# State-space layer: swapped diagonal product, a second home for R, and an output projection one column tile at a time

## The reference, cut to what matters

```
def ssd_mixer(h, w_in, ...):                       # 32 heads of 64, 4 groups of 8 heads, state 128
    z, xbc, dt = split(h @ w_in)
    xs, bm, cm = split(silu(dwconv_centered(xbc)))
    y_f, s_f = ssd_chunked(xs, dt[0], a[0], bm, cm, init_f)
    y_b, s_b = ssd_chunked(flip(xs), flip(dt[1]), a[1], flip(bm), flip(cm), init_b)
    y = y_f + flip(y_b) + xs * d_skip
    y = rmsnorm(y * silu(z), norm_g)
    return y @ w_out, s_f, s_b

def ssd_chunked(x, dt, a, bm, cm, init_state):     # chunks of 128 tokens
    acs  = cumsum(dt * a)
    lmat = exp(where(lower, acs_i - acs_j, -inf))
    wmat = (cc @ bc.T) * lmat * dt
    y_diag = wmat @ xc
    chunk_states = bc.T @ (exp(acs_end - acs) * dt * xc)
    starts = scan(state * exp(acs_end) + chunk_states)
    y_off  = (cc @ starts) * exp(acs)
    return y_diag + y_off, final
```

## Time and profile before

| | us |
|---|---|
| median of 3 runs | 2035.67 (2027.53 to 2037.62) |
| profiled execution | 2033.17 |
| its span, first to last instruction | 2031.3 |
| TensorE busy in it | 1898.1 |
| VectorE, GpSimd, ScalarE busy | 1049.7, 1204.2, 607.1 |

### The profile page before, as it was taken

One profiled execution on the slowest core, in us unless ns is written; L12 is line 12 of the kernel. 1 busy time (PEld: TensorE's weight loads), 2 busy tenths in 40 slices (PEclk: granted clock), 3 DMA queues, 4 the chain that ended last, 5 costly groups with the idle time before them and its releaser, 6 DMA issues. The chain is left out here.

```text
span 2031.3 us, 33370 instructions
## 1 busy us (share of the span) xinstructions
PE 1898.1 (93%) x12777; PEld 1797.1 (88%) x12777; DVE 1049.7 (52%) x1631; ACT 607.1 (30%) x1152; POOL 1204.2 (59%) x869
## 2 busy tenths in 40 slices
PE   4988879999999999989999999986999999999997
PEld 3867768999999999989999899975899999999997
DVE  4445565455246416455675766677426632561553
ACT  4223322122012102233574646474102210220221
POOL 2422325777777677756545555422687767777764
PEclk8989989999999999999999999988999999999998
DMA  8531314242433424433333323221422222222211
GB/s 296 203 116 46 109 34 168 89 154 75 143 108 120 133 85 153 148 104 89 112 94 104 120 78 114 83 77 53 121 73 73 72 71 75 72 73 66 78 56 70
DMA packets 256185, 208.61 MB, mean 103 GB/s; under 512 B 7352, under 2 KB 235741, under 8 KB 255453
## 3 DMA queue, kind: packets, MB, share of 16 engines
q1 hardware_dynamic: 256093, 207.32, 32.3%
HBM read 196.63 MB, written 10.67 MB: 102 GB/s over the span
## 5 line engine op out<-in xcount | busy, mean ns | idle before, releaser
L899 POOL TENSOR_SCALAR w_hi<-raw 128x512 fp32r<-128x512 f32 (+1 forms) x432 | 653.4, 1529 | 801.1 <-PE ps L933 728.0
L903 POOL TENSOR_TENSOR w_lo<-raw,w_hi 128x512 fp32r<-128x512 f32 (+1 forms) x432 | 557.6, 1312 | 0.0
L933 PE MATMUL ps<-h_hi,w_hi 128*128 128x320 f32 (+1 forms) x1688 | 415.0, 326 | 5.2 <-DVE h_lo L2159 3.1
L933 PE MATMUL ps<-h_lo,w_hi 128*128 128x320 f32 (+1 forms) x1688 | 393.4, 314 | 0.0
L933 PE MATMUL ps<-h_hi,w_lo 128*128 128x320 f32 (+1 forms) x1688 | 391.6, 313 | 0.0
L933 PEld LDWEIGHTS ps<-h_hi,w_hi 128*128 128x128 f32 x1688 | 288.0, 192 | 26.5 <-issue 21.2
L933 PEld LDWEIGHTS ps<-h_hi,w_lo 128*128 128x128 f32 x1688 | 289.2, 191 | 0.0
L933 PEld LDWEIGHTS ps<-h_lo,w_hi 128*128 128x128 f32 x1688 | 288.4, 191 | 0.2 <-issue 0.2
L2054 DVE SCALAR_TENSOR_TENSOR xT<-ps,mod,xT 128x128 f32 (+1 forms) x112 | 56.6, 547 | 275.1 <-PE ps L933 269.5
L933 PE MATMUL ps<-g_hi,w_hi 128*128 128x322 f32 (+1 forms) x816 | 190.7, 315 | 7.0 <-DVE g_lo L2115 7.0
L933 PE MATMUL ps<-g_lo,w_hi 128*128 128x322 f32 (+1 forms) x816 | 189.3, 313 | 0.0
(11 more groups left out here) (334 smaller groups left out, 2879.1 us busy)
## 6 DMA issues: line engine op xcount, KB each, us to landing
raw<-in_ffn_w_up SPq DMA_DIRECT2D x88, 512.0 KB, 3.8
ada<-in_ada_w SPq DMA_DIRECT2D x36, 1024.0 KB, 6.4
raw<-in_ssd_w_in SPq DMA_DIRECT2D x40, 512.0 KB, 4.1
R<-scr_acs SPq DMA_DIRECT2D x40, 512.0 KB, 4.7
raw<-in_ffn_w_down SPq DMA_DIRECT2D x32, 512.0 KB, 3.8
ada_att<-in_ada_w SPq DMA_DIRECT2D x12, 1024.0 KB, 8.1
raw<-in_att_w_in SPq DMA_DIRECT2D x16, 512.0 KB, 7.2
raw<-in_ssd_w_out SPq DMA_DIRECT2D x16, 512.0 KB, 3.9
```

Source lines behind the costliest of these rows:

```text
L899: nc.gpsimd.tensor_scalar(w_hi[j % 2][:, a_:b_, :], raw[j][:, a_:b_, :], 1.0, None, ALU.mult).then_inc(w_hi_done, 1)
L903: ins = nc.gpsimd.tensor_tensor(w_lo[j % 2][:, a_:b_, :], raw[j][:, a_:b_, :], w_hi[j % 2][:, a_:b_, :].bitcast(F32), ALU.subtract)
L933: ins = mm(out[:, cols], w[slot][:, k, :], x[:, cols], start=first and k == 0 and i == 0, stop=last and k == n - 1 and i == 2)
```

## The change

Four edits, all in layer 1's mixer.

1. The diagonal product is swapped: 64 columns of xdt are the weights and R moves (128 columns), so the result has channels on partitions, even heads on 0 to 63, odd heads on 64 to 127. y1 (skip term and the two state products) is no longer added by VectorE but multiplied by the identity into the same bank, and the bank goes straight into the gate product. The event yT is gone; yo stands before cb of its chunk, and VectorE makes the skip term there (for chunk 0 in cb).
2. R has a second home: R_mid (in the last four tiles of yg) for odd n up to 13, R_last (in the last four tiles of h_lo's place) for n = 16 and 18. Rows are loaded two chunks ahead; R_last waits for the last projection tile.
3. ScalarE's part of cb is an event of its own, seg, two slots earlier (in the slot of cb for chunk 1 of group 3).
4. Column tiles 2 to 7 of the output projection are done one at a time (both halves of the channels, weight buffers 0 and 1), in PSUM slots m % 4; the sums of squares and the broadcast for the norm stand between the matmuls of tile 2, after k = 1 and k = 5, in banks 6 and 7.

```diff
                 put(*slots[at], "csf", g, c)
+            if c:
+                put(*slots[at - 1], "yo", g, c)
+            put(*slots[at - (0 if (g, c) == (GROUPS - 1, 1) else 2)], "seg", g, c)
             put(*slots[at + 2], "yd", g, c)
-            if c:
-                put(*slots[at + 3], "yo", g, c)
-            put(*slots[at + 6], "yT", g, c)
         put(*slots[10], "stT", g)
...
+        def aligned(at_):
+
+            return -(-at_ // 32) * 32
+
+        R_mid = at("R_mid", [P, 2, GH, P], F32, aligned(g_at + 12 * W * 4))[0]
+        R_last = at("R_last", [P, 2, GH, P], F32, aligned(h_at + 12 * W * 4))[0]
+        N_MID, N_ALL = CHUNKS * (GROUPS - 1), CHUNKS * GROUPS
+
+        def row_home(n):
+
+            if n < N_MID:
+                return (R, R_mid)[n % 2]
+            return (R, R_last)[(n - N_MID) % 2]
+
+        def row_before(n):
+
+            return n - 1 if n == N_MID else n - 2
+
+        def rows_in(n, d_):
+
+            if n < N_MID:
+                return (R_in, RM_in)[n % 2][d_], 16 * (n // 2 + 1)
+            i = n - N_MID
+            return (RL_in[d_], 16 * (i // 2 + 1)) if i % 2 else (R_in[d_], 16 * (-(-N_MID // 2) + i // 2 + 1))
+
         def h2(name, n, offset):
...
                 g, c = divmod(n, CHUNKS)
-                if n and d_ == 0:
-                    sp.wait_ge(R_used, n)
-                elif n:
-                    sp.wait_ge(ssd_mm, SSD_USE[("yd", (n - 1) // CHUNKS, (n - 1) % CHUNKS)] + 1)
+                if n == N_MID + 1:
+                    sp.wait_ge(mm_done, T_E + 40)
+                elif n >= 2:
+                    sp.wait_ge(R_used, 2 * row_before(n) + 1 + d_)
                 src = scr_acs[c, 32 * d_ + g * GH:32 * d_ + (g + 1) * GH, :]
-                sp.dma_start(R[:, d_, :, :], src.partition_broadcast(P)).then_inc(R_in[d_], 16)
+                sp.dma_start(row_home(n)[:, d_, :, :], src.partition_broadcast(P)).then_inc(rows_in(n, d_)[0], 16)
...
                         state_loads(ev[1] + 1)
-                    if ev[0] == "yd" and ev[1:] != (GROUPS - 1, CHUNKS - 1):
-                        for d_ in range(2):
-                            row_loads(CHUNKS * ev[1] + ev[2] + 1, d_)
+                    if ev[0] == "yd":
+                        n = CHUNKS * ev[1] + ev[2]
+                        after = () if n == N_MID - 2 else (n + 1, n + 2) if n in (N_MID - 1, N_MID) else (n + 2,)
+                        for i in after if n != N_MID - 1 else (n + 1,):
+                            for d_ in range(2):
+                                if i < N_ALL:
+                                    row_loads(i, d_)
                     if ev[0] == "stT":
...
                         for r in range(GH):
-                            ins = mm(bank(b, HD, r * HD), R[:, d_, r, :], xdt[:, d_, r * HD:(r + 1) * HD],
-                                     start=(d_, r) == (0, 0), stop=(d_, r) == (1, GH - 1), skip_group_check=True)
-                        ins.then_inc((R_used, ssd_mm)[d_], 1)
+                            half = HD * (r % 2)
+                            ins = mm(bank(b, P, (r // 2) * P)[half:half + HD, :], xdt[:, d_, r * HD:(r + 1) * HD],
+                                     row_home(CHUNKS * g + ev[2])[:, d_, r, :], start=d_ == 0 and r < 2, stop=False, skip_group_check=True)
+                        ins.then_inc(R_used, 1)
+                    pe.wait_ge(y_done, 5 * g + ev[2] + 1)
+                    for q_ in range(4):
+                        ins = mm(bank(b, P, q_ * P), y1[ev[2] % 2][:, q_ * P:(q_ + 1) * P], ident, start=False,
+                                 stop=q_ == 3, skip_group_check=True)
+                    ins.then_inc(ssd_mm, 1)
                 elif kind == "yo":
...
                         mm(bank(b), cT[g % 2][:, cols], src, start=True, stop=True).then_inc(ssd_mm, 1)
-                elif kind == "yT":
-                    pe.wait_ge(y_done, 5 * g + ev[2] + 1)
-                    b = ssd_begin(ev)
-                    for q_ in range(4):
-                        ins = tr(bank(b, P, q_ * P), y1[ev[2] % 2][:, q_ * P:(q_ + 1) * P], ident)
-                    ins.then_inc(ssd_mm, 1)
                 elif kind == "stT":
...
-            def y_rb():
-                pe.wait_ge(yr_dg, 1)
-                rb(diag).then_inc(yr_rb, 1)
-
-            def so_pair(i):
+            def y_sums_row(k):
+
+                if k == 1:
+                    pe.wait_ge(y_added, 15)
+                    for c in range(CHUNKS):
+                        ins = mm(bank(6, 1, c), y_sums[:, chunk_col(c):chunk_col(c) + P], ones[:, 0:1], start=True,
+                                 stop=True)
+                    ins.then_inc(y_ss, 1)
+                if k == 5:
+                    pe.wait_ge(yr_dg, 1)
+                    rb(diag, 6).then_inc(yr_rb, 1)
+
+            def so_tile(m):
                 for part in range(2):
-                    for half in range(2):
-                        pe.wait_ge(w_split, 4 * i + (T_O + 2 * part + half + 1))
-                        if part == 0:
-                            pe.wait_ge(acc_free_dve, 2 * i + (half + dve_accs(A_O) - 2))
-                        steps(half, half, y_of(part), range(KD), first=part == 0, last=part == 1).then_inc(mm_done, 1)
+                    pe.wait_ge(w_split, so_done(m) - 1 + part)
+                    if part == 0:
+                        if m == 2:
+                            pe.wait_ge(*ssd_end(("yd", GROUPS - 1, CHUNKS - 1)))
+                            pe.wait_ge(*ssd_end(("stT", GROUPS - 1, 1)))
+                        elif m == 3:
+                            pe.wait_ge(rbs_done, 1)
+                        else:
+                            pe.wait_ge(acc_free_dve, dve_accs(A_O) + m - 4)
+                    steps(part, so_slot(m), y_of(part), range(KD), first=part == 0, last=part == 1,
+                          after=y_sums_row if (m, part) == (2, 0) else None).then_inc(mm_done, 1)
             for k in range(12, 16):
                 y_part(k)
-            pe.wait_ge(y_added, 15)
-            for c in range(CHUNKS):
-                ins = mm(bank(6, 1, c), y_sums[:, chunk_col(c):chunk_col(c) + P], ones[:, 0:1], start=True, stop=True)
-            ins.then_inc(y_ss, 1)
-            y_rb()
-            with pe.Fori(1, 4) as i:
-                so_pair(i)
+            for m in range(2, KD):
+                so_tile(m)
             ffn(1, T_F1, A_F1)
...
                     A_(st_f[1][:, :] if d_ == 0 else st_b[:, 3, :], bank(b), ACT.Copy).then_inc(ssd_free_act, 1)
-                elif kind == "cb":
+                elif kind == "seg":
                     n = 5 * g + ev[2]
                     c = ev[2]
                     for d_ in range(2):
-                        act.wait_ge(R_in[d_], 16 * (n + 1))
+                        act.wait_ge(*rows_in(n, d_))
+                        R_ = row_home(n)
                         for r in range(GH):
                             i = 32 * d_ + GH * g + r
-                            ins = A_(R[:, d_, r, :], R[:, d_, r, :], ACT.Relu, bias=acs[:, c, i:i + 1], scale=-1.0)
+                            ins = A_(R_[:, d_, r, :], R_[:, d_, r, :], ACT.Relu, bias=acs[:, c, i:i + 1], scale=-1.0)
                         step(ins)
                         step.wait()
-                        A_(R[:, d_, :, :], R[:, d_, :, :], ACT.Exp, scale=-1.0).then_inc(seg_exp, 1)
+                        A_(R_[:, d_, :, :], R_[:, d_, :, :], ACT.Exp, scale=-1.0).then_inc(seg_exp, 1)
                 elif kind == "stT":
...
+            def skip_term(g, c):
+
+                if c >= 2:
+                    dve.wait_ge(ssd_mm, SSD_USE[("yd", g, c - 2)] + 1)
+                elif g:
+                    dve.wait_ge(ssd_mm, SSD_USE[("yd", g - 1, 4)] + 1)
+                return tt(h64(y1[c % 2][:, :]), h64(x_tok[g % 2][:, c, :]), bc(d_bc[:, GH * g:GH * (g + 1)], 2, HD),
+                          ALU.mult)
+
             n_id = 0
...
                     tt(cbm[:, :, :], bc(bank(b, P), 1, 2), masks, ALU.mult).then_inc(ssd_free_dve, 1)
+                    if c == 0:
+                        skip_term(g, 0).then_inc(y_done, 1)
                     if n:
-                        dve.wait_ge(ssd_mm, SSD_USE[("yd", g, c - 1) if c else ("yd", g - 1, 4)] + 1)
+                        dve.wait_ge(R_used, 2 * n)
                     else:
...
                         dve.wait_ge(seg_exp, 2 * n + d_ + 1)
-                        tt(R[:, d_, :, :], R[:, d_, :, :], bc(cbm[:, d_, :], 1, GH), ALU.mult).then_inc(W_done, 1)
+                        R_ = row_home(n)
+                        tt(R_[:, d_, :, :], R_[:, d_, :, :], bc(cbm[:, d_, :], 1, GH), ALU.mult).then_inc(W_done, 1)
                 elif kind == "yd":
-                    n = 5 * g + c
-                    y_ = y1[c % 2][:, :]
-
-                    if c >= 2:
-                        dve.wait_ge(ssd_mm, SSD_USE[("yT", g, c - 2)] + 1)
-                    elif g:
```

(35 more changed lines are left out.)

17 lines of the change are left out of this document (11 added, 6 removed).

## The result

| kernel | median of the runs, us | profiled execution, us | span, us | mean granted clock |
|---|---|---|---|---|
| before, beside it | 2036.64 (4 runs) | 2033.17 | 2031.3 | 0.970 |
| after | 2001.97 (1999.62 to 2008.77, 4 runs) | 1999.62 | 1997.7 | 0.977 |

The ratio is 0.984, with an interval of 0.9815 to 0.9865: faster, by 1.6% and clear of the noise, though by less than 2%. The forecast was 2007.5, in a range of 1996 to 2026; as a ratio, 2007.5/2035.67 = 0.986, just inside the upper end of that interval. The gain in the medians is 34.7 us, in the two profiled executions 33.6, and the forecast had 28.2.

A forecast was written before the change was run, and what follows sets the result against it. TensorE was taken to bound the projection tiles, a chain through several engines the tail. Profiled 2033.2 - 16.8 (product) - 13.4 (tail) + 2 (waits) = 2005.0; with 2.5 for the median 2007.5 us, range 1996 to 2026.

The forecast's parts named there:

- Part 1: Swapped diagonal product on TensorE: column halves overlap, 55 ns a record, burst 1.76 us plus 0.2 for edges, before 3.52.
- rival A: Swapped diagonal product: column halves don't overlap, 107 ns a record, 2035 us in all, no change; chance 0.12.
- The drain at a change of tiling mode: At each swapped burst's edges: 0.11 us seen leaving; at 0.40 an edge the first stretch would win 9 us less.
- Part 2: Identity matmuls replace transposes on TensorE, 0.88 us against 0.44; with the swap 1.12 us won a chunk, 16.8 over fifteen.
- Part 3: New waits in the stretch of projection tiles: +2 us net charged, between -5.5 and +5.
- The walk through the queues: Group 1 in the new order: TensorE held once, 0.3 to 1.5 us, where yo of chunk 4 needs a PSUM bank.
- Rival C: Projection tiles: exponentials ahead of the evacuations hold TensorE, 5.0 us at nine places, 45 in all, 2052 us; chance 0.07.
- Part 4: Tail after the last projection tile: earlier rows shorten the chain through VectorE and GpSimd; 13.4 us won, 2.2 charge included.
- Rival B: Tail keeps its length, held by VectorE or the two weight splits; only the first stretch gains, 2021 us; chance 0.18.
- Part 5: Four PSUM slots for the output projection's last six tiles: alone worth -0.6 to +1.6 us.

The follow-up runs named there:

- one_half: Changed kernel with all sixteen calls of a swapped-product burst writing partitions 0 to 63, output not the reference's; 2025.29 us in one run.
- early_seg: On top of both, the exponentials of chunk 2 of groups 0 to 2 stand two half tiles earlier in ScalarE's queue; 1982.0 us, ratio 0.9739.
- again_2: The changed kernel itself, unedited, run a second further time; 2002.77 us, ratio 0.984 to the kernel before.
- again: The changed kernel itself, unedited, run once more; 2000.97 us, ratio 0.9839 to the kernel before.
- pairs: Changed kernel with output projection column tiles 2 to 7 back in pairs in two PSUM slots, norm's sums and broadcast ahead; 2002.36 us, ratio 0.9847.
- swap_alone: Changed kernel cut to swapped product, identity matmuls and early y1: one home for R, exponentials and row loads as before, tiles in pairs; 2011.13 us, ratio 0.9875.
- same_half: Changed kernel with the swapped product's head order altered to all even heads, then all odd ones; 2017.67 us, ratio 0.9916.
- half_split: Changed kernel with GpSimd splitting in halves the two output projection weight tiles that the last channel tiles need; 2002.44 us, ratio 0.9839.
- early_w: Changed kernel with raw weight loads of four tiles ahead of SyncE's wait for the last gate product and xT; 2008.16 us, ratio 0.9865.
- both: half_split plus the next two weight tiles split in halves and the early raw weight loads of early_w; 1990.32 us, ratio 0.9774.

## Why the prediction was right

Its place in the range follows from its steps, though two errors of about 2 us cancelled in it (parts 2 and 3).

**Part 1, right.** Predicted 1.76 + 0.20 for burst and edges, measured 1.90 and 0.09 for entering. The halves overlap, as the adaLN burst had it; rival A's 107 ns is what one_half shows (114). The drain at a change of tiling mode, which the Trainium skill (TensorEngine Tiling (Array Packing), section Key Properties) brought up against the change, is small here: 0.09 us on entering, and on leaving at most 0.14 (an estimate: 1.90 less 32 records at the prediction's 55 ns). By 0.4 us an edge the sum would be 2.56 instead of 1.99; the trace of this case does not show that.

**Part 2, right, with a small term too small.** The identity records take 0.99 us, not 0.88. A chunk is 3.96 - (0.09 + 1.90 + 0.99) = 0.98 us shorter instead of 1.12, over fifteen 14.7 instead of 16.8.

**Part 3, wrong in place, its size luck in part.** M to T0 fell by 14.7 us, as 16.8 - 2 had it (by 14.6 to 16.0 with the further profiles). By the measured chunk all of that is part 2, so the net charge for waits should have been nothing: that it was 2 made up for the 2.1 too many of part 2. The old waits, 5.5 us in all, went and 6.8 us of new ones came, while 10.2 us of the stretch ran at half clock both before and after. That would leave 13.4 us; where the other 1.3 come from stays open. The walk through the queues found one hold in group 1, at yo of chunk 4; the real one, in each of three groups, is at chunk 2, behind the evacuation of tile cT. And a wait was priced at its own length, while early_seg shows 9.8 us for 6.8. Rival C was thus a true mechanism at a fifth of its price: 9.8 us from three places instead of 45 from nine.

**Part 4, right.** Times after T0:

| step | predicted | measured |
|---|---|---|
| masked R of chunk 1, 2, 3 done | 13.4, 29.3, 44.4 | 13.2, 29.0, 43.9 |
| yout 7, first half done: GpSimd starts | 49.1 | 49.2 |
| chunk 4's burst | 67.8 | 68.3 |
| gate product ends | 71.6 | 72.1 |
| first split for the six tiles done | 87.9 | 88.4 |

From the start of the six tiles to the end of the projection are 89.2 us (1405.51 to 1494.70) against 87.5 before (1435.41 to 1522.94): sums and broadcast among the tiles cost 1.7 net. They take 2.2 themselves, as predicted; the half clock at the start of the tiles ended 3.8 us in instead of 4.6, which gives 0.4 back. In again_2, where it lasted 9.2, the same piece takes 91.7 us. The tail won 15.1 - 1.7 = 13.4, as predicted, and the end of the projection comes 28.2 us earlier, the 28.2 of the sum (27.8 and 27.7 in again and again_2, counted from M). Rival B (the tail keeps its length) is out: the first half of yout 7 did come 7 us earlier.

**Part 5, right by the whole time.** Predicted a gain between -0.6 and +1.6 us; by the medians pairs shows nothing, and in its place the part costs 1.2 to 2.9.

**What the sum did not have.** The profiled executions differ by 33.6 us, 5.4 more than the change's own place. It lies behind it, most of it in the last MLP, in stretches at half clock. The three longest pieces of the chain, before and after:

```profile
1650.45 166.90 PE ps L933 x1110
...
1825.59 138.34 PE ps L933 x918
...
1971.37 40.22 PE ps L933 x258
```

```profile
1622.16 165.38 PE ps L974 x1110
1795.78 136.83 PE ps L974 x918
1940.04 38.70 PE ps L974 x258
```

The same matmuls take 1.5 us less in each, 345.5 against 340.9 us for the three. Other profiles have other numbers of slow pieces: the changed kernel 342.4 in again and again_2, the last experiment's 342.4 as well. But it is not plain chance of an execution either: the three kernels with the tiles in pairs (before, pairs, swap_alone) all have 345.5, and of the eleven others only same_half has. Whether the order of the tiles, or where the layer ends in time, brings these stretches stays open; the interval of the ratio (27 to 38 us) holds both figures.

**A claim that nobody asked for a price.** The prediction took the second home to matter in the tail only and the row loads to be "no engine's bound". For the kernel before, whose y1 came later, no run tests it. Within the change it doesn't hold: with one home the first stretch is 5.2 to 6.6 us longer. Parts of a change should be priced against each other, not only against before.

## What to carry to other kernels

Price a wait on TensorE with the slow clock that follows it, and look at the waits of a stretch together: taking away two of 6.06 and 5.32 us gave 2 to 4 us while one of 6.4 stayed behind them, and 11 to 12.6 us once that went too. Profile the same kernel more than once before a difference of a few microseconds is put down to an edit: here the same place in the tiles lay 1.7 us apart in two profiles of one kernel. When small weights leave part of the array idle, send successive matmuls to different column parts; by turns or two by two is alike, long rows of one part are not. And before long work is put ahead in an engine's queue, look for an idle gap of its length two places further up, and at what evacuates behind it.

## What the runs showed of the hardware that was not expected

- fp32 records with 64 weight columns and 128 moving: 59 ns each by turns between two column halves, 61 two calls by two, 78 four by four, 114 in one half (start to start of 32, with the leaving but not the entering).
- After a wait of 6 to 7 us the tiles ran at a granted clock of 0.50 for 3.3 us in one profile (again, wait of 6.82) and for 9.2 in another of the same kernel (again_2, wait of 6.52); 9.4 in half_split (wait of 6.45) and 9.4 in early_w (wait of 4.76). The length does not follow the wait's; what sets it stays open.
- Waits of 1.25 and 0.99 us in a full stretch cost 3.3 us together (9.8 for three such pairs in the kernel both, where two of the three had half clock behind them), 1.0 more than their length. In the profile after, all three had it, and three pairs cost 11.1.
